# Weight requests of a mixture-of-experts kernel on two queues: the down weights move from SyncE to ScalarE

## What is computed

```python
def expert_block(args):                       # 32 experts, 4 chosen for each token
    tok, e = args
    gu = h[tok] @ w_gate_up[e] + b_gate_up[e]             # 1024 -> 2048
    return clamped_swiglu(gu) @ w_down[e] + b_down[e]     # 1024 -> 1024

y = y * slot_w[:, None]                       # the router's weight of each slot
return zeros_like(h).at[slot_tok].add(y)      # sum over a token's four experts
```

## Time and profile before

| what | value |
|---|---|
| median of 3 runs | 1448.55 us (1445.28 to 1450.72) |
| profiled execution, its own time | 1443.32 us |
| its span, first to last instruction | 1441.5 us |
| mean granted TensorE clock | 0.956 |
| TensorE busy | 1137.9 us, 79% of the span |
| VectorE, ScalarE, GpSimd busy | 286.9, 192.2, 145.8 us |
| queue q1 (SyncE) | 449.71 MB, 80.0% of the 16 engines' span |
| queue q10 (ScalarE) | 8.13 MB, 1.6% |
| queue q0 (GpSimd) | 21.95 MB, 6.0% |

### The profile page before, as it was taken

How to read it: one execution, slowest core, us unless ns; L and a number is a source line. 1 busy time by engine, 2 the same in 40 slices (tenths; PEclk the granted TensorE clock), 3 DMA queues, 4 the chain that set the end, 5 groups by cost and what they waited for, 6 DMA issues and landing times.

```text
span 1441.5 us, 17464 instructions
## 1 busy us (share of the span) xinstructions
PE 1137.9 (79%) x6346; PEld 482.9 (33%) x6346; DVE 286.9 (20%) x658; ACT 192.2 (13%) x491; POOL 145.8 (10%) x212
## 2 busy tenths in 40 slices
PE   3799899982899998787777777777777777777772
PEld 0686477762344442222222222222222222222220
DVE  0111245547111111111111111111111111111113
ACT  1212454120110001010000000100100000000011
POOL 2003000500001100001100000000010000000000
PEclk9999999985899999999999999999999999999996
DMA  9927753621789999999999999999999999999984
GB/s 317 371 75 281 286 187 108 215 88 62 249 309 377 391 372 399 401 401 401 397 395 398 401 399 400 398 400 396 396 401 384 398 394 401 389 403 396 401 345 144
DMA packets 121622, 480.23 MB, mean 333 GB/s; under 512 B 12486, under 2 KB 15782, under 8 KB 104326
## 3 DMA queue, kind: packets, MB, share of 16 engines
q1 hardware_dynamic: 109280, 449.71, 80.0%
q0 software_dynamic: 8592, 21.95, 6.0%
q10 hardware_dynamic: 3718, 8.13, 1.6%
HBM read 471.71 MB, written 15.65 MB: 338 GB/s over the span
## 4 chain that ended last, share of the span: by engine, by line
SPq 46%; PE 29%; DMA 16%; issue 4%; DVE 4%; ACT 1%; ACTq 0%; DVEq 0%; POOLq 0%
SPq L468 33%; DMA ring_r<-in_moe_w 10%; SPq L473 10%; PE ps L1748 6%; PE ps L1438 4%; PE ps L1647 3%; PE ps L1785 3%; PE ps L1410 2%; PE ps L1753 2%; DMA ring<-in_ada_w 2%; DMA ring<-in_moe_w 2%; PE ps L1549 2%; SPq L538 1%; SPq L508 1%; PE ps L1606 1%
## 5 line engine op out<-in xcount | busy, mean ns | idle before, releaser
L1753 PE MATMUL ps<-ring_r,xT 128*64 128x512 f32 x1344 | 331.4, 619 | 133.0 <-DMA ring_r<-in_moe_w 132.8
L1815 PE MATMUL ps<-ring,aT 128*64 128x512 f32 x896 | 214.5, 601 | 34.8 <-DMA ring<-in_moe_w 34.6
L1753 PEld LDWEIGHTS ps<-ring_r,xT 128*64 128x64 f32 x1344 | 86.9, 139 | 361.5 <-DMA ring_r<-in_moe_w 247.8
L1300 DVE TENSOR_SCALAR glu<-ps 128x512 f32<-128x512 f32 (+1 forms) x32 | 23.2, 724 | 660.8 <-PE ps L1753 578.2
L1753 PE MATMUL ps<-ring,xT 128*64 128x512 f32 x448 | 107.4, 602 | 27.4 <-DMA ring<-in_moe_w 27.4
L903 ACT COPY xT<-ps 128x384 f32<-128x384 f32 x66 | 28.4, 482 | 735.0 <-PE ps L1410 735.0
L663 POOL DMA_INDIRECT y_sum<-y_blk,cur_row x32 | 46.2, 1445 | 783.7 <-DVE y_blk L1329 780.3
L1815 PEld LDWEIGHTS ps<-ring,aT 128*64 128x64 f32 x896 | 56.7, 136 | 173.7 <-DMA ring<-in_moe_w 105.4
L1438 PE MATMUL ps<-ring,hm 128*128 128x240 f32 x288 | 64.0, 386 | 3.7 <-ACT hm L727 3.7
L1748 PE MATMUL ps<-ring_r,xT 128*32 128x512 f32 x576 | 64.6, 608 | 0.0
L1753 PEld LDWEIGHTS ps<-ring,xT 128*64 128x64 f32 x448 | 27.8, 136 | 105.8 <-DMA ring<-in_moe_w 70.4
(11 more groups left out here) (269 smaller groups left out, 934.7 us busy)
## 6 DMA issues: line engine op xcount, KB each, us to landing
ring<-in_moe_w SPq DMA_DIRECT2D x192, 1024.0 KB, 20.5
ring_r<-in_moe_w SPq DMA_DIRECT2D x192, 1024.0 KB, 22.3
ring<-in_ada_w SPq DMA_DIRECT2D x24, 1024.0 KB, 14.0
ring<-in_in_w SPq DMA_DIRECT2D x6, 960.0 KB, 13.3
latT<-in_cache_lat_t SPq DMA_DIRECT2D x8, 512.0 KB, 3.7
lat<-in_cache_lat SPq DMA_DIRECT2D x8, 512.0 KB, 4.6
ring<-in_out_w SPq DMA_DIRECT2D x4, 1024.0 KB, 12.2
y_sum<-qabs POOLq DMA_DIRECT2D x5, 384.0 KB, 7.9
```

The source lines that it names most:

```text
L1753: ins = nc.tensor.matmul(ps[half_array(j), r, :], xT[:, kt, 0:SMALL], piece(w[:, j], r), start=False, stop=(kt == GU_UNITS - 1))
L1815: ins = nc.tensor.matmul(y_bank[0][half_array(j), :], aT[:, kt % 4, half_array(kt // 4)], w[:, j * 512:(j + 1) * 512], start=False, stop=( ...
```

## The change

`refill_dn` leaves SyncE's program. SyncE's loop now only asks for gate-up units. ScalarE's program gets a `refill_dn` of its own, called in each of its blocks between the sigmoid and `put_y`: it loads the expert's number, then for each of the four slots waits for the same count of used down units as before and asks for the next unit on ScalarE's queue. Slots, semaphores, sources, waits of TensorE and the loads of block 0 (still asked for by SyncE) stay as they are.

```diff
-        def refill_dn(i, expert):
-
-            for j in range(DN_UNITS):
-                sp.wait_ge(S["dn_unit_used"], dn_used(i - 1, j))
-                load_dn(i, expert, j)
-
         sp.wait_ge(S["table_ready"], 1)
...
         refill_gu(1, expert_of(1))
         with sp.Fori(1, n_ovf + NE - 1) as i:
             refill_gu(i + 1, expert_of(i + 1))
-            refill_dn(i, expert_of(i))
-        refill_dn(n_ovf + (NE - 1), expert_of(n_ovf + (NE - 1)))
         sp.wait_ge(S["y_stored"], (n_ovf + NE) * 16 + 16)
...
+        def refill_dn(i):
+
+            expert = a.value_load(order[0:1, bass.ds(i, 1)], min_val=0, max_val=NE - 1)
+            for j in range(DN_UNITS):
+                a.wait_ge(S["dn_unit_used"], dn_used(i - 1, j))
+                src = moe_w[bass.ds(expert, 1), GU_UNITS + j].rearrange("e p n -> (e p) n")
+                nc.scalar.dma_start(dn_slot(j), src).then_inc(dn_sem[j], 16)
+
         def expert_block(i, wide, wide_before):
             take_x(i + 1)
             swish(i, wide)
+            refill_dn(i)
             put_y(i - 1, wide_before)
             take_act(i, wide)
```

## The result

The changed kernel takes 1462.74 us (median of 4 runs, 1459.55 to 1469.49) against 1448.12 us before (4 runs, 1445.28 to 1450.72). The ratio is 1.0115, 95% interval 1.0087 to 1.0144: slower by 15 us by the medians, 17 us by the ratio. In a second series the ratio was 1.0094 (1.0069 to 1.0119), 13.6 us; both intervals hold 1.010. The forecast was +7.6 us, 1456, with a range up to 1465.

The account below looks back on a forecast made before the run. The prediction took transferred bytes to bound the middle of the expert part. Its terms, 0 for requests, 0 for ScalarE's work and +7.6 us at the end, carried to the median 1448.55, gave 1456 us; range 1446 to 1465.

Parts of the forecast that it names:

- The end: Last block: down 31 is first requested only after the last gate-up unit, at 1406.2 against 1396.13 before; +7.6 us.
- S: Start of the last weight unit's products ahead of down 31's; forecast at 1401.09 us in the profile.
- The middle at zero: Steady blocks: moving four requests per block from SyncE to ScalarE costs 0 us, since bytes set the pace.
- the mixing of two queues: Blocks where both queues hold work, 390 us: 9% less rate would cost 35 us, total 1491; chance 0.10.
- Turns: Each block: queues served in turns; at half the engines four down units land before the next gate-up completes, free in steady part.
- Rival 4: ScalarE's requests wait for SyncE's backlog; y and aT up to 20 us late, covered by 22.50 us idle; no time.
- The levelled end: At the end, two queues level the engines out: S 4.3 us earlier, end term +3.3, 1452; within a shared chance 0.22.
- Nothing to measure: Whole kernel: transfers served in request order over both queues, time stays 1448.5; chance 0.22 together with the levelled end.
- Position: Near the end: start of the last gate-up unit taken as 1401.09, where down 30's last unit started before.

## Why the prediction was right and wrong

- **The end.** Right in mechanism and nearly in size: 7.6 us forecast, 7.8 us timed with ScalarE at the end alone (interval 5 to 11), 8.4 us behind S in the changed kernel's profile and 9.4 to 9.9 in three others. The steps fit too: first request of down 31 at S + 5.1 (1413.79 - 1408.8 = 5.0). From S to the last products it was 18.8 to 20.3 us, not 17.9; the gap ahead of the last unit, where the scatter of y falls, was larger than the 0.4 us I had put there (1.46 us of idle, 2.09 in the run with down 30 alone).
- **The middle at zero.** This is the step that failed ("I cost it at nothing"). It costs 5.9 us (1.0041, interval 1.0020 to 1.0061). I had the mixing of two queues as a bound, read from short stretches early in the kernel, and took it at nothing. For two queues alone that was right: 297.68 MB against 297.70. What I left out is that GpSimd's gather and scatter come in the same microseconds as ScalarE's four units: three queues. The prediction named them only as a part of the 397 against 421 GB/s "which stays".
- **Turns.** I reckoned with half of the engines for ScalarE's queue and had 57.0% in the earlier trace rows. It was 77.2% at the place looked at, in 8 KB pieces against 4 KB ones. The direction was right and the conclusion (down units home before the gate-up) held the more; what I missed is the stop of 6.7 us in the gate-up, and with it TensorE's clock, some 1 us at the end.
- **ScalarE blocked.** Rival 4 fell: 339 to 380 ns for every request.
- **The levelled end.** It fell too: with two queues the engines still run out one after the other, from 0.4 to 0.1 busy between 1400 and 1407 us.
- **Nothing to measure.** The Trainium skill, page "DMA: Bandwidth & Descriptors", section "Issuing engines are not separate DMA queues", says that issuing from several engines saves only the sequencer's time. For the rate of two weight queues alone the traces agree (297.68 and 297.70 MB). As a rule for this change it gave the wrong time: the queues change the order of landing, and that cost 7.8 us, and beside GpSimd's transfers another 5.9.
- **Position.** The start of the last gate-up unit was taken as unchanged, 1401.09. It was 7.7 us later. Of this 1.9 us are the later first sigmoid, which is spread; the rest I put down to the middle and to the slow clock, without a split.

The range held the time, in part by luck: its upper bound of 1465 had 8 us for a loss of two weight queues mixing, which the runs show to be nothing, and this stood in for the 5.9 us that came with GpSimd's transfers. The forecast had half of the difference, because one of two terms was at zero.

## What to carry to other kernels

When this stream of weights in the order of use was split over two queues, the bytes per second stayed (as long as no third queue was busy) and the order of landing did not. So look at the end of the loop, where what used to land last now has landed early and the next request hangs on it. You can test such a term by moving only the last one or two blocks, and only one of their requests: that named the culprit here in two runs. When you cost "two queues at once", count every queue that is busy at that moment, GpSimd's too.

## What the runs showed of the hardware

- Two hardware queues with work do not share evenly: 77.2% of the engines' time for ScalarE's 8 KB pieces, 25.2% for SyncE's 4 KB pieces, 2.57 against 0.80 MB in 8 us, and 341 against 215 pieces.
- The 12 MB that GpSimd's queue moves in gathers and scatters of the small blocks (18 MB as memory counts reads and writes) cost 72 us in a stage bound by transfers (1448.44 to 1376.03). At 413 GB/s they would take 29 us, or 43. A gather's landing goes from 7.4 to 10.6 us when a second weight queue is active.
- Two weight queues alone move what one does, 297.68 and 297.70 MB in 720 us; beside GpSimd's transfers they move 0.5 to 0.7% less.
- After a stop of 6.72 us TensorE's unit of 8 products took 3.68 us instead of 1.94; after stops of 0.6 us as in the earlier trace rows it did not. Idle products of 64 x 512 kept the clock at 1.00 through 15 us; idle products of 32 x 512, also without a stop between them, had a mean of 0.70.
